# A 32-bit embedding product moved from the kernel's end into its pooling stage, and the end cut into five pieces

## The reference, cut to what matters

```python
# layer 0: differential attention (8 heads, context of 256 tokens), layer 1: pooling
x = layer_norm(ALPHA * x + g1 * y_lat, ln_g[i, 0], ln_b[i, 0])      # y_lat: attention or multiscale_pool
x = layer_norm(ALPHA * x + g2 * swiglu(modulate(x, sh2, sc2), ffn_w_in[i], ffn_w_out[i]), ...)
# multiscale_pool: window means less the row itself, in 4 groups of 256 columns
pooled = jnp.stack(outs, axis=2)
y = jnp.einsum('bsgi,gio->bsgo', pooled, w_pool).reshape(B, S, D) * pool_scale
# second block: gated linear attention + block attention, then an MLP, and at the end
x = x + jnp.square(jax.nn.relu(h2 @ w_up)) @ w_down
ple_gate = jax.nn.sigmoid(rms_norm(x, norm_ple) @ w_ple_gate)        # 256x1024 by 1024x1024
x = x + ple_gate * (p @ w_ple)                                       # p is 256x256, w_ple 256x1024
```

## Time and profile before

| | |
|---|---|
| median of 3 runs | 1109.21 us (1108.5 to 1109.56) |
| the profiled execution | 1107.98 us, its span 1106.3 us |
| PE busy | 1091.1 us, 99% |
| DVE, ACT, POOL busy | 776.1 us (70%), 586.3 us (53%), 61.6 us (6%) |
| DMA | 215 GB/s over the span |
| the chain that ended last | PE 88%, DVE 6%, DMA 4%, ACT 1%, issue 1% |

### The profile page before, as it was taken

How to read it: one execution, slowest core, us unless ns; L and a number is a source line. 1 busy time by engine, 2 the same in 40 slices (tenths; PEclk the granted TensorE clock), 3 DMA queues, 4 the chain that set the end, 5 groups by cost and what they waited for, 6 DMA issues and landing times.

```text
span 1106.3 us, 14471 instructions
## 1 busy us (share of the span) xinstructions
PE 1091.1 (99%) x5843; PEld 910.8 (82%) x5843; DVE 776.1 (70%) x1007; ACT 586.3 (53%) x821; POOL 61.6 (6%) x118
## 2 busy tenths in 40 slices
PE   8999999999999999999999999999999999999998
PEld 4788766899998887888888878878888888888886
DVE  2697588889799897877755865455667677874454
ACT  3642366564444347555634767465764466563342
POOL 0011200002121101000000000000000000000000
PEclk8999999999999999999999999999999999999999
DMA  9986840679999946667567788786524456655541
GB/s 364 403 317 229 262 166 1 209 246 332 377 385 355 355 158 228 222 217 255 187 213 131 223 177 188 160 170 139 184 79 153 153 173 211 224 191 190 190 162 39
DMA packets 111986, 238.31 MB, mean 215 GB/s; under 512 B 5712, under 2 KB 51920, under 8 KB 110640
## 3 DMA queue, kind: packets, MB, share of 16 engines
q1 hardware_dynamic: 97280, 185.42, 53.3%
q0 software_dynamic: 14352, 51.72, 13.3%
q10 hardware_dynamic: 288, 0.26, 0.1%
HBM read 236.29 MB, written 1.07 MB: 215 GB/s over the span
## 4 chain that ended last, share of the span: by engine, by line
PE 88%; DVE 6%; DMA 4%; ACT 1%; issue 1%; SPq 0%; ACTq 0%; DVEq 0%
PE ps L2077 18%; PE ps L2078 17%; PE ps L2079 17%; PE ps L2145 10%; PE ps L2147 5%; PE ps L2114 4%; PE ps L2113 4%; PE ps L2112 4%; PE ps L2262 2%; DMA raw<-in_attn_w_qkv 2%; DVE wL L1219 2%; PE ps L2394 1%; PE ps L2362 1%; DMA modraw<-in_mod_rows 1%; DVE modraw L1295 1%
## 5 line engine op out<-in xcount | busy, mean ns | idle before, releaser
L1219 DVE TENSOR_TENSOR wL<-raw,wH 128x1024 fp32r<-128x1024 f32 x326 | 395.0, 1222 | 207.5 <-ACT wH L641 205.1
L641 ACT ACTIVATE wH<-raw 128x1024 fp32r<-128x1024 f32 x326 | 339.9, 1057 | 297.8 <-PE ps L2079 183.2
L2077 PE MATMUL ps<-wH,aHL 128*128 128x512 f32 x576 | 229.7, 399 | 1.0 <-DVE aHL L1627 0.4
L2078 PE MATMUL ps<-wL,aHL 128*128 128x512 f32 (+1 forms) x592 | 229.1, 387 | 0.0
L2079 PE MATMUL ps<-wH,aHL 128*128 128x512 f32 x576 | 224.6, 390 | 0.0
L2145 PE MATMUL ps<-aHL,wH 128*128 128x512 f32 x480 | 168.8, 397 | 0.0
L2077 PEld LDWEIGHTS ps<-wH,aHL 128*128 128x128 f32 x576 | 108.3, 188 | 31.5 <-issue 7.1
L2147 PE MATMUL ps<-aHL,wL 128*128 128x256 f32 x480 | 134.1, 279 | 0.0
L2078 PEld LDWEIGHTS ps<-wL,aHL 128*128 128x128 f32 x592 | 111.5, 188 | 21.3 <-issue 0.5
L2079 PEld LDWEIGHTS ps<-wH,aHL 128*128 128x128 f32 x576 | 108.3, 188 | 23.2
L2145 PEld LDWEIGHTS ps<-aHL,wH 128*128 128x128 f32 x480 | 90.1, 188 | 21.7
(11 more groups left out here) (330 smaller groups left out, 1488.5 us busy)
## 6 DMA issues: line engine op xcount, KB each, us to landing
raw<-in_ffn_w_in SPq DMA_DIRECT2D x88, 512.0 KB
modraw<-in_mod_rows POOLq DMA_DIRECT2D x80, 512.0 KB, 6.9
raw<-in_w_in SPq DMA_DIRECT2D x32, 1024.0 KB
raw<-in_ffn_w_out SPq DMA_DIRECT2D x22, 1024.0 KB
raw<-in_w_up SPq DMA_DIRECT2D x16, 1024.0 KB
raw<-in_w_down SPq DMA_DIRECT2D x16, 1024.0 KB
mod<-in_mod_first SPq DMA_DIRECT2D x8, 1024.0 KB, 16.5
raw<-in_attn_w_qkv SPq DMA_DIRECT2D x8, 1024.0 KB
```

The lines of the kernel that those rows point to most:

```text
L641: nc.scalar.activation(wHigh(n), raw[:, (n // 2) % RAW, (n % 2) * 1024:(n % 2) * 1024 + 1024], ACT.Copy).then_inc(w_hi, 1)
L1219: V.tensor_tensor(wL[:, n % WL, :], raw[:, (n // 2) % RAW, (n % 2) * 1024:(n % 2) * 1024 + 1024], wHigh(n).bitcast(fp32), ALU.subtract).th ...
L2077: T.matmul(outp, xh, h, start=first, stop=False, skip_group_check=part_of)
L2078: T.matmul(outp, xh, l, start=False, stop=False, skip_group_check=part_of)
```

## The change

**The embedding product** is computed in the pooling stage by plain 32-bit matmuls, with p transposed on the host (`p_cols`). POOL's queue loads w_ple and that p into the space in which `hH` will lie later, once 16 of the 22 pieces of the first w_out are used. Where the fillers stood PE does `embed`: four matmuls for token tile 0, one and three for tile 1; two fillers stay and read `hL`. ACT copies each tile from PSUM (`ple_copy`), POOL's queue stores both, 1 MB, to device memory (`embedded`), and ACT's `high(5)` in the second network waits for that store, because the copied product lies where `hH` is written then. Near the end POOL's queue reads 1 MB back (`plv`) where it read p before.

**The end.** The gate product is now the last product, its tile 1 by column halves. ACT, DVE and SP take it in five pieces (`LAST`): two halves of tile 0, one half of tile 1 and two quarters.

**Also in the diff**, and not named above: in the first modulation steps the split of piece 6 comes behind the row copy of step 3, on ACT and DVE; in the qkv stage the Silu of `cb` and the first `heads_out` come ahead of the split of piece 16, and the second `heads_out` right behind it.

```diff
...
+
+LAST = ((0, 0, 512), (0, 512, 1024), (1, 0, 512), (1, 512, 768), (1, 768, 1024))
...
         sF = ExitStack()
+        sPle = ExitStack()
+        wple = sb(sPle, "wple", [P, 2, D])
+        pT_ = sb(sPle, "pT_", [P, 2, S])
+        pout = sb(sPle, "pout", [P, TT, D])
+        sPle.close()
...
         sE = ExitStack()
-        pt = sb(sE, "pt", [P, TT, 256])
-        pH = sb(sE, "pH", [P, 2, S], f32r)
-        pL = sb(sE, "pL", [P, 2, S], f32r)
+        plv = sb(sE, "plv", [P, TT, D])
...
             rows_of(SUBS["pg"], a["w_ple_gate_2"][0], 0, KT)
-            rows_of(SUBS["ple"], a["w_ple_2"][0], 0, 2)
-            for i in range(4):
-                t, lo = i // 2, i % 2 * CW
+            for i, (t, lo, hi_) in enumerate(LAST):
                 sp.wait_ge(x_done, i + 1)
-                sp.dma_start(out[0, t * P:(t + 1) * P, lo:lo + CW], x[:, t, lo:lo + CW]).then_inc(out_done, 16)
-            sp.wait_ge(out_done, 16 * 4)
+                sp.dma_start(out[0, t * P:(t + 1) * P, lo:hi_], x[:, t, lo:hi_]).then_inc(out_done, 16)
+            sp.wait_ge(out_done, 16 * len(LAST))
...
                 .then_inc(pool_in, 16)
+            pool.wait_ge(w_used, SUBS["out0"] + 16)
+            pool.dma_start(wple[:, :, :], a["w_ple_2"][0].rearrange("(k p) n -> p k n", p=P)).then_inc(ple_in, 16)
+            pool.dma_start(pT_[:, :, :], a["p_cols"]).then_inc(ple_in, 16)
...
             vec_load(IN_FF0)
+            pool.wait_ge(ple_out, TT)
+            pool.dma_start(embedded, pout[:, :, :]).then_inc(ple_stored, 16)
...
             pool.wait_ge(w_used, summed("down"))
-            pool.dma_start(pt[:, :, :], a["p_2"][0, 0].rearrange("(t p) d -> p t d", p=P)).then_inc(p_in, 16)
+            pool.wait_ge(ple_stored, 16)
+            pool.dma_start(plv[:, :, :], embedded).then_inc(p_in, 16)
...
             for c in range(NMOD0):
-                if c == 3:
-                    adv(2 * c)
...
                 mod_copy(c)
-                if c < 3:
-                    adv(2 * c)
+                adv(2 * c)
...
                 adv(j)
+            act.wait_ge(cb_in, 16)
+            nc.scalar.activation(cb[:, :], cb[:, :], ACT.Silu).then_inc(cb_ready, 1)
...
             for c in range(2, 6):
                 for j in range(3):
+                    if (c, j) == (2, 0):
+                        heads_out(0)
                     adv(n + 4 * c + WS + j)
                     if (c, j) == (2, 0):
-                        act.wait_ge(cb_in, 16)
-                        nc.scalar.activation(cb[:, :], cb[:, :], ACT.Silu).then_inc(cb_ready, 1)
-                    if (c, j) == (2, 1):
-                        heads_out(0)
-                    elif (c, j) == (2, 2):
                         heads_out(1)
                     elif c in (3, 4) and j == 2:
                         heads_out(c - 1)
...
                         act.wait_ge(gated_done, c - 1)
+                        if c == 5:
+                            act.wait_ge(ple_stored, 16)
...
+            def ple_copy(t):
+                act.wait_ge(ple_done, t + 1)
+                nc.scalar.activation(pout[:, t, :].rearrange("p (b c) -> p b c", b=2),
+                                     (pair(UNITS["pool"] + 1) if t == 0 else ps[:, 6:8, :]), ACT.Copy).then_inc(ple_out, 1)
...
                     .then_inc(t_hi, 1)
+            ple_copy(0)
...
             ln_x3()
+            ple_copy(1)
...
             rms(2, acc_out, UNITS["down"] + 1, "rms2")
-            adv(SUBS["ple"])
-            hi(GROUPS["p"], pH[:, :, :])
-            adv(SUBS["ple"] + 1)
-            for t in range(TT):
-                un = UNITS["pg"] + t
+            for t, lo, hi_ in LAST:
...
                     act.wait_ge(tile0_done, TILE0["pg"])
+                elif lo == 0:
+                    act.wait_ge(half_done, 2 * TT + 1)
...
                     act.wait_ge(w_used, summed("pg"))
-                nc.scalar.activation(gate[:, t, :].rearrange("p (b c) -> p b c", b=2), pair(un), ACT.Sigmoid)\
-                    .then_inc(acc_out, 1)
+                nc.scalar.activation(gate[:, t, lo:hi_], pair(UNITS["pg"] + t)[:, lo // CW, lo % CW:lo % CW + hi_ - lo],
+                                     ACT.Sigmoid).then_inc(gate_done, 1)
...
             for c in range(NMOD0):
-                if c == 3:
-                    adv(2 * c)
                 mod_put(c)
-                if c < 3:
-                    adv(2 * c)
+                adv(2 * c)
...
             rms(2, "rms2", "down", "pg")
-            adv(SUBS["ple"])
-            lo(GROUPS["p"], pL[:, :, :], pH[:, :, :], k_hi=hcount[0])
-            adv(SUBS["ple"] + 1)
-            for i in range(4):
-                t, b = i // 2, i % 2
-                columns = slice(b * CW, (b + 1) * CW)
-                if b == 0:
-                    dve.wait_ge(half_done, 2 * TT + t + 1)
-                else:
-                    product_done("ple", t)
-                dve.wait_ge(acc_out, UNITS["pg"] + t + 1)
+            dve.wait_ge(p_in, 16)
+            for i, (t, lo_, hi_) in enumerate(LAST):
+                columns = slice(lo_, hi_)
+                dve.wait_ge(gate_done, i + 1)
                 gt = gate[:, t, columns]
-                link(V.tensor_tensor(gt, pair(UNITS["ple"] + t)[:, b, :], gt, ALU.mult))
+                link(V.tensor_tensor(gt, plv[:, t, columns], gt, ALU.mult))
...
                 for _ in range(count):
-                    T.matmul(ps[:, bank, :], hH[:, 0, 0:P], hH[:, 2:4, :], start=True, stop=True)
+                    T.matmul(ps[:, bank, :], hL[:, 0, 0:P], hL[:, 2:4, :], start=True, stop=True)
...
+            def embed(t, bank, steps):
+                for i in steps:
+                    b, k = i // 2, i % 2
+                    ins = T.matmul(ps[:, bank + b, :], pT_[:, k, t * P:(t + 1) * P], wple[:, k, b * CW:(b + 1) * CW],
+                                   start=k == 0, stop=k == 1)
+                    if i == 3:
+                        ins.then_inc(ple_done, 1)
...
                 if t == 1:
-                    idle_mm(10, 3)
+                    pe.wait_ge(ple_in, 32)
+                    embed(0, 2 * ((UNITS["pool"] + 1) % 2), range(4))
...
             for t in range(TT):
-                if t == 0:
+                if t == 1:
+                    pe.wait_ge(ple_out, 1)
+                else:
...
-            idle_mm(2)
+            embed(1, 6, range(1))
             x3_groups(0)
-            idle_mm(5)
+            embed(1, 6, range(1, 4))
...
-            def p_group():
-                pe.wait_ge(p_in, 16)
-                group(GROUPS["p"], [pt[:, t, k * P:(k + 1) * P] for k in range(2) for t in range(TT)])
-
-            rows_mm(SUBS["pg"], UNITS["pg"], aH, aL, KT, GROUPS["rms2"],
-                    hooks={(5, 0): tile_ready("rms2", xn, xn_ready, 3 * TT), (1, 1): p_group})
-            pe.wait_ge(t_lo, GROUPS["p"] + 1)
-            rows_mm(SUBS["ple"], UNITS["ple"], pH, pL, 2, GROUPS["p"], halves=(0, 1))
+            rows_mm(SUBS["pg"], UNITS["pg"], aH, aL, KT, GROUPS["rms2"], halves=(1,),
+                    hooks={(5, 0): tile_ready("rms2", xn, xn_ready, 3 * TT)})
```

More of the change, by code:

```diff
@@ L66 @@
                       ("win", 64), ("bra", 8), ("brb", 8), ("wo2", 8), ("up", 32), ("down", 32), ("pg", 8),
-                      ("ple", 2)):
+                      ):
     SUBS[_name] = _n
@@ L76 @@
                       ("in1", 20), ("out1", 2), ("win", 16),
-                      ("bra", 2), ("brb", 2), ("wo2", 2), ("up", 14), ("down", 2), ("pg", 2), ("ple", 2)):
+                      ("bra", 2), ("brb", 2), ("wo2", 2), ("up", 14), ("down", 2), ("pg", 2)):
     UNITS[_name] = _n
@@ L85 @@
                       ("pool", 4), ("x3", 4), ("in1", 2), ("rms0", 4), ("glaA", 2), ("mqk", 8), ("oa", 4),
-                      ("ob", 4), ("y", 4), ("rms1", 4), ("up", 4), ("rms2", 4), ("p", 1)):
+                      ("ob", 4), ("y", 4), ("rms1", 4), ("up", 4), ("rms2", 4)):
     GROUPS[_name] = _n
@@ L161 @@
 WIN = (0, 2, 1) + tuple(range(3, 16))
-TILE0 = {name: i + 1 for i, name in enumerate(("wo", "out0", "pool", "out1", "bra", "brb", "wo2", "down", "pg", "ple"))}
+TILE0 = {name: i + 1 for i, name in enumerate(("wo", "out0", "pool", "out1", "bra", "brb", "wo2", "down", "pg"))}
 SUB_OF = (("q", "qkv", 4, 0), ("k", "qkv", 4, 8), ("v", "qkv", 4, 16), ("wo", "wo", 0, 4), ("in0", "in0", 4, 0),
@@ L168 @@
           ("win", "win", 4, 0), ("bra", "bra", 0, 4), ("brb", "brb", 0, 4), ("wo2", "wo2", 0, 4), ("up", "up", 4, 0),
-          ("down", "down", 0, 28), ("pg", "pg", 0, 4), ("ple", "ple", 0, -2))
+          ("down", "down", 0, 28), ("pg", "pg", 0, 4))
 def summed(stage, j=0):
@@ L409, in build @@
         p_in, x_done, out_done = sem("p_in"), sem("x_done"), sem("out_done")
+        ple_in, ple_done, ple_out, ple_stored, gate_done = (sem(n) for n in
+                                                            ("ple_in", "ple_done", "ple_out", "ple_stored", "gate_done"))
         def pair(un):
@@ L437, in build @@
```

(17 more changed lines are left out.)

## The result

The changed kernel takes 1099.05 us, the median of 4 executions (1098.37 to 1099.22), against 1108.86 for the kernel before: ratio 0.9912, 95% interval 0.9898 to 0.9925. A second comparison, 1099.32 against 1108.29, gave 0.9926 (0.9908 to 0.9945).

A forecast was written before the change was run, and what follows sets the result against it. The prediction took TensorE (PE), busy 99% of the span, to bound the kernel. Its terms -1.68 + 1.40 - 5.87 + 0.60 = -5.55 us took the median from 1109.21 to 1103.7 us, range 1101.6 to 1106.2.

The forecast's parts named there:

- A: Order on ACT in the qkv stage: removes PE's idle gap before the second query heads' transposes, -1.68 us.
- The move of one split and one DVE step: At the start, behind the copy of the last modulation rows: put at 0, between -0.1 and +0.5 us.
- The term that I did put down: Qkv stage: Silu and first-heads copy ahead of the DMA-held split close PE's gap from 66.97 to 68.88, -1.68 us.
- B: Embedding product in the pooling stage: plain 32-bit matmuls at 0.88 us each replace fillers, +1.40 us.
- The first place: Pooling stage: four plain matmuls replace ten fillers, mostly inside PE's wait for DVE, +0.17 us.
- The store: 1 MB store awaited by ACT before hH of chunk 5: lands in 6 to 9 us, cost 0; slow-store rival 4%.
- C: The end: matmuls and transposes of p removed, -5.87 us; tail after the last matmul longer, +0.6 us.
- new wait at the head transposes: Rival, qkv stage: PE's gap only changes its name, waiting for something else; 1105.4 us, chance 12%.
- dearer pooling: Rival, pooling stage: 0.97 us a matmul (+0.8) and one ACT copy on the path (+1); 1105.5 us, chance 11%.
- clock fall in the pooling stage: Rival: granted clock falls to 1.2 GHz there, eight matmuls take twice as long, +7; 1110.7 us, chance 3%.
- late read-back: Rival, the end: DVE waits for the read-back, up to 5.3 us come back; 1109.0 us, chance 2%.
- the likeliest case: The forecast by itself, whole kernel: from 1102.3 (pooling 0.5, tail 0.4) to 1104.8 us (0.97 a matmul, tail 0.8); 66%.

The follow-up runs named there:

- f4: The changed kernel with ten, two and five fillers in place of the plain 32-bit matmuls, embedding product left out: 1099.95 us against 1099.32 for the changed kernel.
- e1: The kernel before, unchanged, run again for its profile: 1108.54 us, ratio 1.0007.
- e3: The changed kernel with the order on ACT and DVE in the modulation and qkv stages as before, split of piece 6 included: 1102.91 us.
- f2: The kernel before with three plain 32-bit filler matmuls added behind the second modulation step as a delay: 1107.67 us, ratio 0.9998 to the kernel before.
- g1: The kernel before with the new end alone, embedding product left out (the gate multiplies the input x): 1102.03 us, ratio 0.9945.
- g2: The kernel before with the new pooling stage alone, old end kept and nothing read back: 1108.22 us against 1107.91, ratio 1.0.
- f3: The changed kernel with three plain 32-bit filler matmuls added behind the second modulation step as a delay: 1100.51 us against 1099.32.
- e4: The kernel before with only the split of weight piece 6 moved behind the last modulation row copy, on ACT and DVE: 1108.0 us, ratio 1.0.
- e2: The kernel before with only the new order on ACT and DVE in the modulation and qkv stages: 1105.55 us, ratio 0.9974.
- f1: The changed kernel, unchanged, run again for its profile and more executions: 1099.32 us.
- g4: The changed kernel with the end in four pieces, tile 1's last half in one: 1099.6 us.
- h2: The kernel before with only the new order on ACT and DVE, second of four further profiled executions: 1105.63 us.
- h4: The kernel before with only the new order on ACT and DVE, fourth of four further profiled executions: 1107.66 us.

## Why the prediction was wrong

**A, the step that failed.** "The move of one split and one DVE step behind the copy of the last modulation rows, at the start, I put at 0 (ACT's slack there is idle time of more than a split)." That slack, 0.86 us for PE, is real only in an execution in which PE is late, as in the one I had read: its second modulation step began at 20.92 us, that of the other seventeen profiles at 18.0 to 19.0 in all but one (f4). Of the six profiles without the move (before, e1, e3, f2, g1, g2) the four in which PE is neither late nor delayed have a wait of 0.97 to 1.27 us for the row copy, and in three of these (e1, g1, g2) the granted clock then stands at half for about 3 us. None of the twelve with the move has either there. Leaving out the late and the delayed ones (before, f2, f3, f4), the first transposes stand at 60.54 on average without the move and 59.42 with it: 1.1 us that my sum had at nothing. By itself the move gains nothing (e4), since the copy of the query heads swallows what comes early; only both together bring it.

The term that I did put down, "66.97 to 68.88 loses 1.91 - 0.23 = -1.68", was right in its mechanism: Silu and copy ran where I had put them, and nothing new holds PE. Its size was near the average, but by luck, since one execution can show much more or less. The gap is no fixed loss but the difference between two clocks. One is the DMA's: in seven profiles with the copy in its old place (before, e1, e3, e4, f2, g1, g2) the second transposes stand at 68.56 to 69.16. The other is PE's: in all with the new order it is 6.5 us after the first transposes, 65.36 to 66.46 where PE is not late or delayed. So an earlier PE only widens the gap. In the same four profiles without the move, the second transposes come 7.68 to 9.45 us after the first, so the gap is worth 1.2 to 2.95, 1.8 on average. The two parts, 1.8 and 1.1, are 2.9 by the traces; e2 measured 2.9 (1.0 to 4.9). How the 2.9 divides is read from traces alone: no run has the new order of the copies without the move. I had what I needed for both: each time an urgent copy stood behind a split that waits for a DMA, and such a wait has to be priced over the range of arrival times of the engine that waits.

**B was too dear.** The price of the plain matmul was right, 0.885 against 0.88. The Trainium skill (TensorE: Matmul & The Clock Gate, "Why this matters for your kernels") says that a single matmul on 32 rows takes as long as on 128, so the earlier trace rows could stand for this one. The trace agrees: 0.885 here, 0.85 to 0.91 by that row. The first place takes 404.17 - 400.63 = 3.54 us against 406.38 - 403.03 = 3.35: +0.19, forecast +0.17, and a wait of 0.38 for DVE's sh stands ahead of it (0.34 in e1, ahead of the fillers). But by the first half product of the second network PE stands 0.96 us later than at the windows product, compared with before, 0.93 in f1 and 0.31 in g2 and g4, and g2's time is the same as before to 0.1%. The sum had put nearly all of PE's added time on the path, +1.40; the traces show 0.3 to 1.0 of it, and by time it can't be told from 0. I had kept such a return for the range's end.

**The store** cost nothing, as forecast: 7.0 us to landing, ACT 0.41 late, PE's matmuls unbroken. The Trainium skill (DMA: Bandwidth & Descriptors, "Anatomy of one DMA — SWDGE (gpsimd) path") has a formula by which 1 MB takes 4.4 us, an estimate, and warns of stores to HBM. Here the store took 7.0 and the load of the same bytes 5.1, at different times, both longer than the estimate. The loads and the read-back were hidden.

**C was right but for 0.3.** Counted from the last half product, at 985.47 before and 982.21 after, the last matmul starts 5.94 us earlier (forecast 5.87), and the span's tail is 0.40 longer (0.60). Measured alone the end is worth 6.1 (4.2 to 8.0).

**The remainder.** Measured one by one, the parts are 2.9, 0 and 6.1, about the whole's 9 to 9.8. By the traces they are -2.9, +0.3 to +0.96 and -5.5, about -8. The intervals of the two comparisons reach from 6.1 to 11.3, so the rest is not clear of noise. One thing beside the change may add to it. The slow pair in the second network, 1.7 us, was in before, e4, h2 and h4 and half of it in g2, five of ten profiles with the old end, and in none of the eight with the new one; at that rate it would be worth nearly 0.8 us on average. What ties it to the end of the program, if anything does, I don't know; only the coincidence is shown, and no experiment singles out a cause.

Of the rivals none came: no new wait at the head transposes (the one near 48 us lies ahead of the first ones and is counted in their times), no dearer pooling, no clock fall in the pooling stage (1.00 throughout), no late read-back. The range failed because I bounded A at what one execution showed, as if it could only shrink. The ends of the likeliest case were added up wrongly as well: by its own terms it runs from 1102.6 to 1104.7.

## What to carry to other kernels

A wait that ends at a DMA is a nearly fixed point in time: what removing it is worth depends on how early the waiting engine can be, so look at several executions, or delay the engine and see whether the delay is swallowed, and at which place. Where two such points follow each other, removing the first alone can measure as nothing (e4). An in-order engine that does urgent copies between operations that wait for DMAs should do the copies first. And time added to PE in a stage with waits right behind it is not all paid.

## What was not expected of the hardware

The same matmuls, with no idle time and the granted clock at 1.00, followed each other at 0.355 us a pair in some executions and 0.349 in others, in one stage alone; the other stage with the same two lines has 0.3517 in all of them. Idle gaps of PE of 1.01 to 1.27 us at the last modulation step (e1, g1, g2) and one of 2.67 us (e4) were followed by the lower clock level for about 3 us; one of 0.97 at the same step and one of 2.79 at the second transposes (both e3) were not: there the transposes took 1.06.
